# A 128-token triangular solve done as forward substitution over two 64-token blocks

## The reference, cut to what matters

```python
def _rwkv7_scan(r, w, k, v, za, zb):
    def step(S, inp):
        r_t, w_t, k_t, v_t, a_t, b_t = inp
        sa = jnp.einsum("bhij,bhj->bhi", S, a_t)
        S = S * w_t[:, :, None, :] + sa[..., None] * b_t[:, :, None, :] + v_t[..., None] * k_t[:, :, None, :]
        return S, jnp.einsum("bhij,bhj->bhi", S, r_t)
    ...
    _, ys = lax.scan(step, S0, xs)
```

## Time and profile before

| what | value |
|---|---|
| median of three runs | 737.7 us (736.28 to 738.16) |
| time of the profiled execution | 735.89 us |
| span of the profiled execution | 734.1 us |
| granted TensorE clock, mean | 0.998 |
| busy share PE / PEld / DVE / ACT / POOL | 99% / 80% / 76% / 59% / 7% |
| matrix instructions | 7266 |

### The profile page before, as it was taken

How to read it: one execution, slowest core, us unless ns; L and a number is a source line. 1 busy time by engine, 2 the same in 40 slices (tenths; PEclk the granted TensorE clock), 3 DMA queues, 4 the chain that set the end, 5 groups by cost and what they waited for, 6 DMA issues and landing times.

```text
span 734.1 us, 16878 instructions
## 1 busy us (share of the span) xinstructions
PE 723.1 (99%) x7266; PEld 589.8 (80%) x7266; DVE 561.1 (76%) x895; ACT 434.1 (59%) x688; POOL 49.5 (7%) x83
## 2 busy tenths in 40 slices
PE   9999999999999999999999999999999999999997
PEld 6888878888788888888878685898888888865553
DVE  6689978777789999997668788899685676763453
ACT  5689973425748666766547562487573755653342
POOL 0000133040020000000002000003003000000000
PEclk9999999999999999999999999999999999999999
DMA  9990205330776655665771732348335354466001
GB/s 344 377 394 22 111 18 222 128 103 17 239 229 220 220 182 178 226 229 174 283 291 43 287 141 106 117 142 318 116 133 212 112 213 171 195 229 240 19 1 58
DMA packets 64171, 129.52 MB, mean 176 GB/s; under 512 B 1889, under 2 KB 24929, under 8 KB 63713
## 3 DMA queue, kind: packets, MB, share of 16 engines
q1 hardware_dynamic: 63056, 126.06, 48.0%
q0 software_dynamic: 320, 1.67, 0.7%
q10 hardware_dynamic: 720, 0.71, 0.3%
HBM read 127.39 MB, written 1.05 MB: 175 GB/s over the span
## 4 chain that ended last, share of the span: by engine, by line
PE 84%; DVE 9%; DMA 3%; ACT 2%; issue 1%; SPq 0%; DVEq 0%
PE bank L628 38%; PE bank L750 14%; PE bank L3204 11%; DMA ring<-in_w_in_dram 3%; PE bank L2524 3%; PE bank L1564 3%; PE bank L1545 2%; DVE arena L574 1%; PE bank L885 1%; PE bank L1822 1%; DVE arena L1127 1%; PE bank L2001 1%; DVE arena L616 1%; PE bank L2741 1%; PE bank L3027 1%
## 5 line engine op out<-in xcount | busy, mean ns | idle before, releaser
L628 PE MATMUL bank<-hg,arena 128*128 128x256 f16 x2496 | 275.0, 273 | 0.2 <-DVE hg L653 0.2
L628 PEld LDWEIGHTS bank<-hg,arena 128*128 128x128 f16 x2496 | 243.9, 98 | 30.5 <-issue 1.1
L574 DVE SCALAR_TENSOR_TENSOR arena<-ring,arena 128x1024 f16<-128x1024 f32 x150 | 175.5, 1226 | 59.3 <-ACT arena L542 59.3
L542 ACT ACTIVATE arena<-ring 128x1024 f16<-128x1024 f32 x150 | 146.7, 1044 | 86.9 <-PE bank L3204 37.6
L3204 PE MATMUL bank<-arena 128*128 128x512 f16 (+1 forms) x480 | 83.6, 336 | 0.0
L3204 PEld LDWEIGHTS bank<-arena 128*128 128x128 f16 x480 | 47.0, 98 | 36.1
L750 PE MATMUL bank<-arena 128*128 128x256 f16 x528 | 57.8, 273 | 0.0
L750 PEld LDWEIGHTS bank<-arena 128*128 128x128 f16 x528 | 51.7, 98 | 6.0
L561 DVE SCALAR_TENSOR_TENSOR arena<-ring,arena 128x2048 f16<-128x2048 f32 x22 | 50.4, 2292 | 0.7
L750 PE MATMUL bank<-mix,arena 128*128 128x256 f16 x384 | 42.2, 273 | 0.0
L554 ACT ACTIVATE arena<-ring 128x2048 f16<-128x2048 f32 x22 | 41.7, 1895 | 0.0
(11 more groups left out here) (415 smaller groups left out, 961.4 us busy)
## 6 DMA issues: line engine op xcount, KB each, us to landing
ring<-in_w_in_dram SPq DMA_DIRECT2D x12, 2048.0 KB, 11.0
ring<-in_ffn_w_up_dram SPq DMA_DIRECT2D x22, 1024.0 KB, 7.8
ring<-in_w_ff_dram SPq DMA_DIRECT2D x8, 2048.0 KB, 9.6
ring<-in_w_ff_dram SPq DMA_DIRECT2D x16, 1024.0 KB, 6.6
ring<-in_ffn_w_down_dram SPq DMA_DIRECT2D x11, 1024.0 KB, 6.3
ring<-in_w_out_dram SPq DMA_DIRECT2D x8, 1024.0 KB, 7.7
ring<-in_w_xk_dram SPq DMA_DIRECT2D x2, 2048.0 KB, 12.7
ring<-in_w_xv_dram SPq DMA_DIRECT2D x2, 2048.0 KB, 10.8
```

The costliest lines, as they stand in the source:

```text
L542: nc.scalar.activation(quarter(halves_of(chunk)[0], chunk, q), quarter(slot(*chunk), chunk, q), ACT.Copy, scale=W_SCALE).then_inc(*mark("w ...
L574: nc.vector.scalar_tensor_tensor(quarter(halves_of(chunk)[1], chunk, q), quarter(slot(*chunk), chunk, q), W_SCALE, quarter(halves_of(chunk ...
L628: mm = nc.tensor.matmul(out_, weight[a][:, k, cols], src[:, k, b, :], start=(first and i == 0), stop=(last and i == 2), skip_group_check=True)
```

## The change

Both solves stop at the inverses of the 64-token blocks. `XT128` and `X64` go, and with them L1917, L1928, L1940, L2085, L2089, L2100 and POOL's copies L2201. In their place stands `XT64`, which holds the two 64x64 inverses of a head above each other. `AK` gets a buffer of its own, since `LT` is needed later.

The solve is then: the first 64 rows of `G` are copied out, `solved(0, g)` gives the first 64 rows of `U`, these are copied out, multiplied by `LT[0:64, j, 64:128]` and accumulated onto the last 64 rows of `G` ("second G bank"), these are copied out, and `solved(1, g)` gives the last 64 rows of `U`. The order on PE becomes AK, RK, `fill(12)`, `G`, `y_products(0)`, `solved(0)`, RB, second G, `fill(14)`, `solved(1)`, then in chunk 0 the value part of the state, `y_products(2)`, the `U` part of the state and `base_products(1)`, and in chunk 1 `y_products(1)` and `y_products(2)`. `fill(10)` stays in front of AK. On ACT the two copies of `G` and two of `U` of a chunk become eight, of 64 partitions each, at the same place of its list. DVE's and POOL's lists are otherwise as before.

```diff
@@ -406,7 +406,7 @@
                 P=[view(p, 4, BASE // 2), view(p + 64, 4, BASE // 2)], P32=view(a + 896, 4, BASE),
-                XT128=view(a + 1024, 4, C), X64=view(a + 1536, 4, 64), RK=view(rk, 4, C),
+                XT64=view(a + 1024, 4, 64), AK=view(a + 1280, 4, C), RK=view(rk, 4, C),
                 ARB=view(a + 2304, 4, C), G=view(a + 2816, 4, 64), U=view(a + 3072, 4, 64))
@@ -1914,33 +1914,12 @@
                                       tile_position=(64 * i + BASE, 64 * i))
-            mm = nc.tensor.matmul(banks[3 * g + 1][BASE:64, BASE * j:BASE * j + BASE], st["XT"][BASE:64, j, :],
-                                  st["P32"][BASE:64, j, :], start=True, stop=True,
-                                  tile_position=(BASE, BASE))
         mm.then_inc(*mark("solve_pe", "dX32 bank", c, g))
...
     for g in range(2):
-        st = sets[g]
-        pe.wait_ge(*at("X64", c, g))
-        pe.wait_ge(*at("X64 diagonal", c, g))
-        for j in range(4):
-            mm = nc.tensor.matmul(banks[3 * g][64:128, 64 * j:64 * j + 64], st["LT"][0:64, j, 64:128],
-                                  st["X64"][0:64, j, :], start=True, stop=True)
-        mm.then_inc(*mark("solve_pe", "P64 bank", c, g))
-
+        pe.wait_ge(*at("XT64", c, g))
     products(c, 1, KT_, AT_, "AK bank")
-    fill(11)
-    for g in range(2):
-        st = sets[g]
-        pe.wait_ge(*at("P64", c, g))
-        pe.wait_ge(*at("XT diagonal", c, g))
-        pe.wait_ge(*(at("y scaled", 3) if c else at("gate out", g)))
-        for j in range(4):
-            mm = nc.tensor.matmul(banks[3 * g + 2][0:64, 64 * j:64 * j + 64], P64[g][64:128, j, :],
-                                  st["XT128"][64:128, j, 64:128], start=True, stop=True)
-        mm.then_inc(*mark("solve_pe", "dXT64 bank", c, g))
-
     if c == 0:
@@ -1949,7 +1928,7 @@
-            mm = nc.tensor.matmul(banks[3 * g + 1][:, 64 * j:64 * j + 64], sets[g]["LT"][:, j, :],
+            mm = nc.tensor.matmul(banks[3 * g + 1][:, 64 * j:64 * j + 64], sets[g]["AK"][:, j, :],
                                   VTOK[:, c, 64 * hd:64 * hd + 64], start=(j == 0), stop=(c == 0),
@@ -1964,25 +1943,57 @@
+    def y_products(n):
+        for j in range(4):
+            for g in range(2):
+                st, lo, hd = sets[g], 64 * g, 2 * j + g
+                left, right = ((VTOK[:, c, 64 * hd:64 * hd + 64], st["RK"][:, j, :]),
+                               (s0c[lo:lo + 64, j, :], RT_[lo:lo + 64, j, C:2 * C]),
+                               (st["U"][:, j, :], st["ARB"][:, j, :]))[n]
+                mm = nc.tensor.matmul(quarters(3 * g)[lo:lo + 64, j, :], left, right,
+                                      start=(n == 0 and j == 0), stop=(n == 2), skip_group_check=True)
+                if n == 2 and j == 3:
+                    mm.then_inc(*mark("solve_pe", "y bank", c, g))
+
+    def solved(i, g):
+        st, q = sets[g], slice(64 * i, 64 * i + 64)
+        for j in range(4):
+            mm = nc.tensor.matmul(banks[3 * g + 1][q, 256 + 64 * j:320 + 64 * j], st["XT64"][q, j, :],
+                                  st["G"][q, j, :], start=False, stop=True, skip_group_check=True)
+        mm.then_inc(*mark("solve_pe", ("first U bank", "U bank")[i], c, g))
+
     for g in range(2):
-        pe.wait_ge(*at("XT64", c, g))
+        pe.wait_ge(*at("RK", c, g))
+    y_products(0)
+    for g in range(2):
+        pe.wait_ge(*at("first G", c, g))
+        pe.wait_ge(*at("XT diagonal", c, g))
+        solved(0, g)
+    for g in range(2):
+        pe.wait_ge(*(at("y scaled", 3) if c else at("gate out", g)))
     products(c, 2, BT, RT_, "RB bank")
-    fill(13)
     for g in range(2):
         st = sets[g]
-        pe.wait_ge(*at("G", c, g))
+        pe.wait_ge(*at("first U", c, g))
         for j in range(4):
-            mm = nc.tensor.matmul(banks[3 * g + 1][:, 256 + 64 * j:320 + 64 * j], st["XT128"][:, j, :],
-                                  st["G"][:, j, :], start=True, stop=True)
-        mm.then_inc(*mark("solve_pe", "U bank", c, g))
+            mm = nc.tensor.matmul(banks[3 * g + 1][64:128, 64 * j:64 * j + 64], st["LT"][0:64, j, 64:128],
+                                  st["U"][0:64, j, :], start=False, stop=True, skip_group_check=True)
+        mm.then_inc(*mark("solve_pe", "second G bank", c, g))
     fill(14)
     for g in range(2):
-        pe.wait_ge(*at("U", c, g))
-        pe.wait_ge(*at("RK", c, g))
+        pe.wait_ge(*at("G", c, g))
+        solved(1, g)
+    if c:
+        y_products(1)
+    for g in range(2):
         pe.wait_ge(*at("RB", c, g))
...
                                            (BTOK, lambda g, j: sets[g]["U"][:, j, :]))):
+            if n:
+                for g in range(2):
+                    pe.wait_ge(*at("U", c, g))
+                y_products(2)
             for j in range(4):
@@ -1991,20 +2002,11 @@
                         mm.then_inc(*mark("solve_pe", "state bank", g))
-    for n in range(3 if c else 2):
...
-    if c == 0:
         base_products(1)
-    fill(15)
+    else:
+        for g in range(2):
+            pe.wait_ge(*at("U", c, g))
+        y_products(2)
@@ -2079,27 +2081,16 @@
             e = slice(64 * i, 64 * i + BASE)
...
+            nc.vector.tensor_copy(st["XT64"][e, :, BASE:64],
                                   banks[3 * g + 1][e, 128:128 + 4 * BASE].rearrange(
-                                      "p (j n) -> p j n", j=4)).then_inc(*mark("solve_vector"))
-        nc.vector.tensor_copy(st["X64"][BASE:64, :, 0:BASE], banks[3 * g + 1][BASE:64, 0:4 * BASE].rearrange(
-            "p (j n) -> p j n", j=4)).then_inc(*mark("solve_vector", "X64", c, g))
-    for g in range(2):
-        dve.wait_ge(*at("P64 bank", c, g))
-        nc.vector.tensor_copy(P64[g][64:128, :, :],
-                              banks[3 * g][64:128, 0:256].rearrange("p (j m) -> p j m", j=4)).then_inc(
-            *mark("solve_vector", "P64", c, g))
+                                      "p (j n) -> p j n", j=4)).then_inc(
+                *mark("solve_vector", *(("XT64", c, g) if i else ())))
     mem_low(dve, 4 * c + 4)
...
         dve.wait_ge(*at("AK bank", c, g))
-        nc.vector.tensor_tensor(sets[g]["LT"], quarters(3 * g + 1), over(const("strict"), 4),
+        nc.vector.tensor_tensor(sets[g]["AK"], quarters(3 * g + 1), over(const("strict"), 4),
                                 ALU.mult).then_inc(*mark("solve_vector", "AK", c, g))
-    for g in range(2):
-        dve.wait_ge(*at("dXT64 bank", c, g))
-        nc.vector.tensor_copy(sets[g]["XT128"][0:64, :, 64:128],
-                              banks[3 * g + 2][0:64, 0:256].rearrange("p (j m) -> p j m", j=4)).then_inc(
-            *mark("solve_vector", "XT64", c, g))
     for g in range(2):
@@ -2162,16 +2153,18 @@
         act_y_scaled(act)
...
+    for i in range(2):
+        q = slice(64 * i, 64 * i + 64)
+        for g in range(2):
+            st = sets[g]
+            act.wait_ge(*at(("G bank", "second G bank")[i], c, g))
+            nc.scalar.activation(st["G"][q], banks[3 * g + 1][q, 0:256].rearrange("p (j m) -> p j m", j=4),
+                                 ACT.Copy).then_inc(*mark("solve_act", ("first G", "G")[i], c, g))
+        for g in range(2):
+            st = sets[g]
+            act.wait_ge(*at(("first U bank", "U bank")[i], c, g))
+            nc.scalar.activation(st["U"][q], banks[3 * g + 1][q, 256:512].rearrange("p (j m) -> p j m", j=4),
+                                 ACT.Copy).then_inc(*mark("solve_act", ("first U", "U")[i], c, g))
     if c:
@@ -2187,8 +2180,7 @@
         for g in range(2):
-            nc.gpsimd.memset(sets[g]["X64"], 0.0).then_inc(*mark("solve_pool"))
-            nc.gpsimd.memset(sets[g]["XT128"], 0.0).then_inc(*mark("solve_pool", "inverses zeroed", g))
+            nc.gpsimd.memset(sets[g]["XT64"], 0.0).then_inc(*mark("solve_pool", "inverses zeroed", g))
     for g in range(2):
@@ -2196,15 +2188,9 @@
             pool.wait_ge(*at("inverses zeroed", 1))
...
         for b in range(4):
-            q = slice(BASE * b, BASE * b + BASE)
-            nc.gpsimd.tensor_copy(st["XT128"][q, :, q], st["XT"][q, :, :]).then_inc(
+            q, o = slice(BASE * b, BASE * b + BASE), BASE * (b % 2)
+            nc.gpsimd.tensor_copy(st["XT64"][q, :, o:o + BASE], st["XT"][q, :, :]).then_inc(
                 *mark("solve_pool", *(("XT diagonal", c, g) if b == 3 else ())))
```

More of the change, by code:

```diff
@@ L1993, in pe_rwkv_chunk @@
                                 mm.then_inc(*mark("solve_pe", "state bank", g))
-            for n in range(3 if c else 2):
-                for j in range(4):
-                    for g in range(2):
-                        st, lo, hd = sets[g], 64 * g, 2 * j + g
-                        left, right = ((VTOK[:, c, 64 * hd:64 * hd + 64], st["RK"][:, j, :]),
-                                       (st["U"][:, j, :], st["ARB"][:, j, :]),
-                                       (s0c[lo:lo + 64, j, :], RT_[lo:lo + 64, j, C:2 * C]))[n]
```

(44 more changed lines are left out.)

## The result

| kernel | median of its runs | before on the same chip | ratio, 95% interval |
|---|---|---|---|
| after the change | 737.66 us (22 runs) | 736.47 us (22 runs) | 1.0018, 1.001 to 1.0025 |

The change makes the kernel 0.18% slower, 1.3 us. The forecast was 0.45%, 3.3 us. The sign was right, the size was not. The profiled execution took 737.73 us against 735.89 before, its span 735.9 against 734.1.

The account below looks back on a forecast made before the run. PE was taken as the bound (84% of the chain), with new waits outweighing its lighter work: 2.3 us in chunk 0 plus 1.0 in chunk 1, 3.3 slower, 737.7 to 741.0 us (0.45%); range 736.6 to 743.0.

Parts of the forecast that it names:

- PE work, 0.7 us less per solve: PE in each solve: 3.87 us of products removed, 3.21 added, so 0.7 us less per solve, 1.4 in all.
- Copies of 64 partitions at 0.38 us: ACT's copies of G and U: each priced at 0.38 us, like the 128-partition copy with as many columns.
- Chunk 1, 1.0 us lost: End of chunk 1: the late last U copy delays splits and `y out`, turning 0.7 us gained into 1.0 lost.
- the order of events as written: Chunk 1: last U copy, two `w_out` splits on ACT, DVE's low half, `y out`, then PE's transpose at 173.85.
- Nothing absorbs a delay: Behind each solve: a delay of PE is passed on whole, since a stage that PE alone fills follows.
- Chunk 0, 2.3 us lost: End of chunk 0: chunk 1 begins at 138.8 in place of 136.45, 2.3 us later.
- both waits: Chunk 0: PE idles some 1.5 us before the first `solved` and 1.4 us before chunk 1.
- So `G` leaves ACT where it does now: Chunk 0: ACT copies G behind the `w_out` splits, which start at the 126.06 landing; first group out at 128.34.
- The hand-overs: Between engines: 0.3 us from PE's last issue to ACT, 0.24 from a copy's end to PE, 0.25 to DVE.
- The median of before: Starting time of the sum: 737.7 us, to which 3.3 us was added for 741.0.
- The drain rule: PE: changing the tiling mode drains the engine; 0.2 us was put at `solved(1)`, behind the mem part.
- The 0.21 us before P64: PE in the old order: 0.21 us of idle before P64, read as a price between groups of different shape.

Follow-up runs that it names:

- all3: The changed kernel with chunk 0's ACT splits between the copies, both state parts before `y_products(2)`, and chunk 1's splits moved ahead; median 734.65 us, ratio 0.9979.
- act_c0: The changed kernel with chunk 0's two `w_out` splits on ACT moved behind the first U and second G copies; ratio 1.0022 on before.
- split_c1: The changed kernel with chunk 1's `w_out` splits moved into ACT's gaps and DVE's first low half ahead of the keys; ratio 1.0004 on before.
- late_after: The changed kernel with the two transfers of `w_out` rows 0 issued about 3 us later; ratio 1.0103 on before.
- late_before_2: Second profile of the kernel before with the two `w_out` transfers issued about 3 us later; measured 741.07 us.

## Why the prediction was right in its mechanism and wrong in its size

- **PE work, 0.7 us less per solve.** Right. `solved` and second G took 1.07 to 1.08 us each as priced from P64. Chunk 1 brings PE to w_out 0.79 us sooner (171.83 - 155.59 against 171.63 - 154.60). In all3, with the waits gone, the stretches are 0.50 and 0.80 shorter than before's.
- **Copies of 64 partitions at 0.38 us.** Right, a single one took 0.38 (act_c0 and all3).
- **Chunk 1, 1.0 us lost.** Right: 0.85 (24.12 against 23.27), with the order of events as written, and split_c1 takes it back.
- **Nothing absorbs a delay.** Right: 556.2 us behind it in all traces.
- **Chunk 0, 2.3 us lost.** This step failed. It measured 0.81 and 1.09 in two traces of after, and 0.26 where the landing didn't bite. Its mechanism, both waits, was right. Two terms were too large. *"So `G` leaves ACT where it does now"*: I took one profiled execution's landing (6.73 us after mem part 5, the latest of the six that were issued at the old place) as the kernel's; the drawn 5.98 made 0.75 us of the difference, and an early one makes the wait vanish. *The hand-overs*, some 0.8 us in all: from `solved(1)` to `y_products(2)` I had 0.9 us and it took 0.60; from the last state product to chunk 1 I had 2.06, and it took 1.78; from L594 to `solved(0)` I had 2.52, and it took 2.32. I had put 0.3 from PE's last issue to ACT and 0.24 from the end of a copy to PE. Behind `solved(1)` the last copy of `U` started 0.11 us after PE's next group (133.65 against 133.54), ended at 134.03, and PE went on at 134.14, 0.11 later; and DVE began the state scaling 0.07 us after PE's next group (135.73 against 135.66), where I had 0.25. Two lags read at one place in the old order were used for every hand-over of the new one.

```profile
133.65 0.38 ACT L2166 ACTIVATE arena<-bank 64x256 f32<-64x256 f32 x1
```

- **The size over runs.** 0.26 + 0.85 = 1.1 us with an early landing and 1.7 to 1.9 with the two profiled ones; the measured 1.3 has an interval of 0.7 to 1.8 that holds both. So the timed runs don't say which landing is the common one. Of the six traces with the issue at the old place two landed within 5.4 us. That act_c0 won nothing in the median would fit a commonly early landing; no run shows it.
- **The median of before** in the table I started from, 737.7 of three runs, was high; 22 runs have 736.47. Setting my sum on it added 1.2 us to the time that I named.
- **The drain rule** (the Trainium skill, "TensorEngine Tiling (Array Packing)", Key Properties), which I had priced at 0.2 us per solve: gaps of 0.17 and 0.21 us stand at some of the new changes of shape (before `solved` in act_c0 0.17, behind the mem part 0.21). At others none shows: after's rows have no idle from `solved` to RB at 128.89 (64x64 to 64x128) nor from RB to the second G at 129.98 (back). So the trace agrees with the rule only in part, a gap per change of shape is too high a price, and the gaps don't decide. The 0.21 us before P64, which I had read as such a gap, has DVE's copy L2082 as its releaser in the earlier trace rows.

## What to carry to other kernels

When a change splits one dependent step into several, list for each engine what stands in its program order between the new first and the new last hand-over; work that used to sit harmlessly behind the step now delays it, and moving that work into the gaps can turn the loss into the gain. Price a wait that ends on a transfer over several executions, not from one, since that row is a draw. And cut traces at starts that both kernels share: here stretches into which no draw enters repeat to 0.01 us, where the start alone scatters by 2.2.

## What the runs showed of the hardware that I had not expected

- The granted clock can fall to its 1.2 GHz level behind one short idle of PE: it did after 2.95, 1.52 and 1.44 us, and did not after 2.33, 1.70 or 1.14 us in other executions. From mem part 5 to the mem part before AK in chunk 1 the fall cost about 3.1 us in late_after (41.41 - 36.08, less 2.2 of longer idle) and 3.2 in late_before_2 (39.80 - 36.23, less 0.3). What decides, no run shows. In the first and the last of these the DMA share was about 1.05 when the clock fell; in the second, in split_c1, it was near zero. There PE stopped for 1.52 us well ahead of anything that was edited, and the clock fell:

```profile
106.87 0.13 PEld L1889 LDWEIGHTS bank<-arena 32*32 32x32 f32 x2 [1.52 <-issue]
108.00:110.00 2.00, 2.00 (x8) 0.50 0.00 0
```

- That stop and that fall are where split_c1's late start comes from: at 99.2 us it stood level with before, at mem part 5 it was 2.0 us behind. The plain kernel's scatter looks like such falls too, though none of its traces has one there: of the 35 runs of before that were timed beside act_c0, seven have a mean granted clock of 0.997 and take 737.4 to 738.6 us, and the other 28 have a median of 736.05.
- One transfer pair, issued at the same point of the program, took 7.5 to 9.5 us to be used in six executions, though the issue stood 2.7 us ahead of mem part 5 in each. What makes the difference, no run shows.
- DVE's fp16 split L1523 took 2.34 us before and 1.33 after. POOL's two-input L2273 ran beside it before (121.29 to 123.64), and after, as L2259, it was over at 122.44. The first lines are of before, the second fence is of after.

```profile
121.29 2.35 POOL L2273 TENSOR_TENSOR arena<-arena 128x1024 f32<-128x1024 f32 x1
...
122.38 2.34 DVE L1523 SCALAR_TENSOR_TENSOR sqs<-ring,sqs 128x1024 f16<-128x1024 f32 x1
```

```profile
120.09 2.35 POOL L2259 TENSOR_TENSOR arena<-arena 128x1024 f32<-128x1024 f32 x1
...
122.19 1.33 DVE L1523 SCALAR_TENSOR_TENSOR sqs<-ring,sqs 128x1024 f16<-128x1024 f32 x1 [1.58 <-ACT sqs L1516]
```
